# Two-layer hybrid mixer on one core: layer 1's input stage moved into the block of layer 0's output projection

## The chip, the cores and the metric

One core of a Trainium2 chip runs the whole program in one launch. The metric is the device time of one execution in microseconds (us), lower is better. TensorE is called PE here, its weight loads PEld, VectorE DVE, ScalarE ACT, GpSimd POOL, and SyncE, which only issues transfers, SP.

## What is computed

Two layers run over 1152 tokens of 1024 channels: 1024 latent tokens and 128 context tokens. Attention and delta rule couple the tokens inside a layer. Cut to what matters here, a layer is:

```python
mod = (jnp.dot(jax.nn.silu(cond), w_mod) + b_mod)[:, None, :]
shift, scale, gate = jnp.split(mod, 3, axis=-1)
h = rmsnorm(x, norm_pre) * (1 + scale) + shift
z = jnp.einsum('bld,de->ble', h, w_in)        # 2832 columns
... pooling, attention and delta branches of z ...
y = jnp.einsum('ble,ed->bld', gates * branches, w_out)
x = x + gate * rmsnorm(y, norm_post)
```

`cond` is `c` for latent tokens and `c_ctx` for context tokens. It is an input, so the modulation of layer 1 does not depend on layer 0. `h` of a token depends only on that token's `x`, so the input stage of layer 1 can work on a tile of 128 tokens as soon as layer 0 has finished that tile.

## The kernel before

The tokens are 9 tiles of 128, and three groups of 384 (`GRP`). Every matrix product in f32 accuracy is made of three passes over a high and a low part (`split3`, lines 88 to 96), so one output unit of 128 channels by 384 tokens takes 8 blocks of the contraction times 3, 24 matmuls. Order is written out by hand: each engine runs its instructions in the order of the code and waits on semaphores.

A loop on the chip (`Fori`) runs over the two layers. A layer consists of two blocks, with a barrier and a clearing of semaphores after each:

* `enter` (line 114), the input stage. SP loads the x tiles (`load_x`: from the inputs for layer 0, from `out_y` in DRAM for layer 1, chosen by a branch) and four 2 MB blocks of `w_mod`, in the order of `LOADS`. For each tile, ACT squares and sums it (L683), POOL makes the reciprocal root (L283 to L285), DVE scales it (L446), PE turns it by 8 transposes (L562) and ACT copies it to `h_f32` (L691). In between PE multiplies the blocks of `w_mod` (`mod_product`, L547; each row is copied by DVE at L450 and turned by PE at L553). Only when shift and scale are there, DVE modulates (L458), ACT rounds the high part (L696) and DVE subtracts the low part (L465); PE starts the products of `w_in` behind the first low part. Those go through 11 chunks of columns (`CHUNKS`). The first four chunks have 6 units each, numbered n = 0 to 23; the token-major chunks follow with 9 units each, and then 24 gate units. ACT empties each unit from PSUM (L719 and others) out of a ring of six banks. The last two blocks of `w_mod` (the gate vector) are products 4 and 5: PE does them behind units 3 and 8, and their turns behind unit 13 (`extra`). They share one buffer `wg`. DVE splits each weight chunk (L361, L363) and does the six convolutions (L370, L373).
* `mix_and_project` (line 775): delta rule, scan, attention, and `project_out` (line 1819). There PE runs 48 matmuls of 512 columns for each token tile (L2015). ACT squares and sums the result (L1942), POOL makes the root (L1962, L1964), DVE scales by root and gate (L1983), POOL adds x (L1968), and SP stores the tile to `out_y`. The last tile is done in two halves (L1937, L1939, L1978, L1981).

`io["y"]` has a place for each layer, so layer 1 loads in `enter` what layer 0 stored, and loads it once more in `project_out` for the addition.

## Time and profile before

| what | us |
|---|---|
| median of 3 runs | 1774.92 |
| lowest and highest of them | 1767.24, 1775.39 |
| the profiled execution's own time | 1763.57 |
| its span, first to last instruction | 1761.9 |
| PE busy | 1640.4 (93% of the span) |
| DVE, POOL, ACT busy | 1000.7, 923.4, 622.0 |
| PE's last product of layer 0 ends | about 872.5 from the start |
| PE's first `w_in` product of layer 1 starts | 935.19 from the start |

The span is read in order: layer 0's input stage from 5 to 348, its delta rule, scan and attention to about 770, its output projection to 877, and then layer 1 with the same stages. Only one core runs. The profiled execution was 11 us shorter than the median of the runs, so a sum made against the trace has to be moved before it is compared with a median.

### The profile page before, as it was taken

The page shows a single profiled execution, that of the slowest core. Times are in us where ns is not written, and L with a number is a line of the kernel's source. Part 1 is how long each engine was busy: PE and PEld are TensorE (multiplying, and loading weights), DVE is VectorE, ACT ScalarE, POOL GpSimd, SP SyncE. Part 2 cuts the span into 40 slices and gives each one's busy share as a digit, 9 for nine tenths or more (in the row PEclk, how much of TensorE's full clock was granted, in tenths as well). Part 3 has the DMA queues.
Part 4 walks back from the last instruction along what each step waited for, and adds up shares of the span by engine and source line. Part 5 has one row for each costly group of instructions (what it writes and reads, how often), then busy time and mean ns, then how long its engine had stood idle before and what let it go on. Part 6 is the DMA issues. An engine that isn't in the chain of part 4 may idle for free. (4 is left out here: it accounts for less than half of the span.)

```text
span 1761.9 us, 40485 instructions
## 1 busy us (share of the span) xinstructions
PE 1640.4 (93%) x17250; PEld 1342.9 (76%) x17250; DVE 1000.7 (57%) x1472; ACT 622.0 (35%) x1260; POOL 923.4 (52%) x856
## 2 busy tenths in 40 slices
PE   4999999989989999999849999999999899999998
PEld 2899999979976555558628999999799765555586
DVE  2672246377746767791126722463777477677911
ACT  4412321144444444561143123211444444445611
POOL 1003594089944878852210035940899448788522
PEclk8999999999999999999969999999999999999999
DMA  9312013110000001032292220131100000010322
GB/s 335 112 68 77 25 62 102 54 41 22 4 12 14 7 26 33 26 138 100 80 321 102 74 77 25 61 102 55 42 22 4 12 14 7 26 33 26 138 99 81
DMA packets 71246, 117.22 MB, mean 67 GB/s; under 512 B 10128, under 2 KB 42128, under 8 KB 71056
## 3 DMA queue, kind: packets, MB, share of 16 engines
q1 hardware_dynamic: 70128, 114.18, 19.1%
q8 instruction: 140, 2.29, 0.5%
q10 hardware_dynamic: 928, 0.34, 0.1%
q14 instruction: 50, 0.41, 0.1%
HBM read 95.03 MB, written 19.47 MB: 65 GB/s over the span
## 5 line engine op out<-in xcount | busy, mean ns | idle before, releaser
L1439 POOL TENSOR_TENSOR attn_accp<-attn_accp,attn_pr 128x1024 f32<-128x1024 f32 x110 | 269.4, 2449 | 42.3 <-ACT attn_pr L1505 36.6
L93 PE MATMUL ps<-h_hi,in_w_hi 128*128 128x384 f32 x768 | 261.0, 340 | 5.0 <-DVE h_lo L465 4.9
L94 PE MATMUL ps<-h_lo,in_w_hi 128*128 128x384 f32 x768 | 259.3, 338 | 0.0
L95 PE MATMUL ps<-h_hi,in_w_lo 128*128 128x384 f32 x768 | 259.1, 337 | 0.0
L1709 DVE TENSOR_REDUCE attn_ql<-ps 128x1 f32<-128x1152 f32 x128 | 172.6, 1355 | 102.3 <-PE ps L1627 102.0
L1505 ACT ACTIVATE attn_pr<-ps 128x512 f32<-128x512 f32 x292 | 158.7, 595 | 170.7 <-PE ps L1671 162.0
L93 PEld LDWEIGHTS ps<-h_hi,in_w_hi 128*128 128x128 f32 x768 | 145.0, 189 | 10.1 <-issue 6.7
L1670 PEld LDWEIGHTS ps<-attn_QH,attn_KH 128*128 128x128 f32 x292 | 55.5, 190 | 122.1 <-ACT attn_pr L1505 55.2
L94 PEld LDWEIGHTS ps<-h_lo,in_w_hi 128*128 128x128 f32 x768 | 145.2, 189 | 0.0
L95 PEld LDWEIGHTS ps<-h_hi,in_w_lo 128*128 128x128 f32 x768 | 145.1, 189 | 0.0
L1680 PE MATMUL ps<-attn_pr,z 128*64 128x512 f32 x520 | 139.5, 615 | 0.0
L919 POOL TENSOR_TENSOR delta_ML<-delta_EK,local 128x256 f32<-128x256 f32 x180 | 130.6, 746 | 14.2 <-PE ps L957 13.5
L1670 PE MATMUL ps<-attn_QH,attn_KH 128*128 128x512 f32 x292 | 131.5, 450 | 0.0
L93 PE MATMUL ps<-in_w_hi,h_hi 128*128 128x256 f32 (+1 forms) x432 | 124.1, 287 | 0.0
L95 PE MATMUL ps<-in_w_hi,h_lo 128*128 128x256 f32 (+1 forms) x432 | 122.7, 284 | 0.0
L94 PE MATMUL ps<-in_w_lo,h_hi 128*128 128x256 f32 (+1 forms) x432 | 122.5, 283 | 0.0
L957 PE MATMUL ps<-delta_TR,delta_ML 64*64 64x64 f32 x2880 | 111.0, 221 | 11.0 <-POOL delta_ML L919 5.0
L1671 PE MATMUL ps<-attn_QL,attn_KO 65*128 65x512 f32 x292 | 116.2, 398 | 0.0
L297 POOL TENSOR_TENSOR in_scratch<-zz 128x1175 f32<-128x1175 f32 x4 | 8.6, 2144 | 201.2 <-ACT zz L721 201.2
L957 PEld LDWEIGHTS ps<-delta_TR,delta_ML 64*64 64x64 f32 x2880 | 97.3, 135 | 18.7 <-DVE delta_TR L1199 11.8
L1199 DVE TENSOR_TENSOR delta_TR<-delta_TR,ps 128x256 f32<-128x256 f32 x180 | 72.7, 404 | 52.2 <-PE ps L957 50.3
L1627 PE MATMUL ps<-attn_KH,attn_QH 128*128 128x384 f32 x384 | 89.6, 341 | 1.9 <-DVE attn_ql L1709 1.9
(251 smaller groups left out, 3581.3 us busy)
## 6 DMA issues: line engine op xcount, KB each, us to landing
in_w<-in_w_in SPq DMA_DIRECT2D x22, 1024.0 KB, 5.4
zz<-in_w_mod SPq DMA_DIRECT2D x8, 2048.0 KB, 12.9
gates<-in_gate SPq DMA_DIRECT2D x48, 192.0 KB, 1.9
z<-out_y SPq DMA_DIRECT2D x18, 512.0 KB, 5.2
attn_gt<-gates SPq DMA_DIRECT2D x34, 256.0 KB, 2.7
z<-in_x_sample SPq DMA_DIRECT2D x16, 512.0 KB, 5.2
z<-in_w_mod SPq DMA_DIRECT2D x4, 2048.0 KB, 10.1
out_w<-in_w_out SPq DMA_DIRECT2D x16, 512.0 KB, 6.0
```

The source lines that it names most:

```text
L93: nc.tensor.matmul(out, a_hi(i), b_hi(i), start=(i == 0), stop=False)
L94: nc.tensor.matmul(out, a_hi(i), b_lo(i), start=False, stop=False)
L95: last = nc.tensor.matmul(out, a_lo(i), b_hi(i), start=False, stop=(i == n - 1))
L919: nc.gpsimd.tensor_tensor(pairs(ML[d][:, i % 2]), EA[d][:, j % 3, :, 0], level_mask(i, d), ALU.mult).then_inc(ml_done, 1)
L957: last = nc.tensor.matmul(heads(bank, off)[rows(c), h, :], lhs(rows(c), h), rhs(rows(c), h), start=True, stop=True)
L1439: nc.gpsimd.tensor_tensor(acc, a, pr[:, n % 4], ALU.add).then_inc(pool_added, 1)
L1505: nc.scalar.activation(pr[:, n % 4, e], ps[:, e, :], ACT.Exp, scale=HD ** -0.5).then_inc(p_done, 1)
L1627: last = nc.tensor.matmul(ps[:, bank + c, 0:GRP], QH[:, p % 3, blk // 2, col:col + P], KH[:, g, GRP * c:GRP * c + GRP], start=True, stop=True)
L1670: nc.tensor.matmul(ps[:, e, :], KH[:, g, ks], QH[:, p % 3, e, :], start=True, stop=False)
L1671: nc.tensor.matmul(ps[:, e, :], KO[0:HD + 1, g, ks], QL[0:HD + 1, p % 2, e, :], start=False, stop=True).then_inc(st_done, 1)
L1680: nc.tensor.matmul(ps[HD * e:HD * e + HD, 2 + p % 2, :], values(p, kt, e), pr[:, n % 4, e], start=(kt == 0), stop=(kt == STEPS_OF[p] - 1)) ...
L1709: nc.vector.tensor_reduce(ql[:, a % 4, blk, HD:HD + 1], ps[:, bank:bank + 3, 0:GRP], AX_XY, ALU.max).then_inc(mx_read, 1)
```

## The change

The loop over the layers is written out in Python. Layer 0 still has an input block of its own (`enter`, l = 0). Layer 1's input stage becomes a set of functions which run in the block of layer 0's `project_out`, as `nxt`:

* While PE multiplies tile t of layer 0's output projection, tile t - 2 is turned. ACT squares the finished y tile where it lies in SBUF, POOL makes the root, DVE scales it into one buffer `xn`, PE does its 8 transposes inside product t (behind block k = 1; in the last product behind block k = 3 of the first half), and ACT copies it to the h buffers. DVE modulates group 0 behind tile 3 and group 1 behind tile 6. The first weight chunk of layer 1 is loaded at tile 3 and split behind tile 4.
* Shift, scale and gate of layer 1 are made in layer 0's input stage: products 6 to 11 of 2 MB blocks of `w_mod`, one behind each of the units 10, 13, 16, 19, 21 and 23, through the one buffer `wg`. The turns go behind units 9, 15, 20 and 25. Product 5 moves from unit 8 to unit 7.
* Layer 1's first chunk is done as `side_by_side`: for each block k, both channel blocks of a token group. The high and low parts are made only after the last output product, since they lie where its operands lay. The last two tiles are turned inside groups 0 and 1, and the two halves of the last y tile are scaled and added between low parts. ACT instead of DVE rounds the high part of chunk 1.
* Layer 1 no longer loads y in its input stage, nor `w_mod`.

```diff
-    names = " ".join(f"x{i}" for i in range(1, len(ap.shape)))
-    return ap[bass.ds(l, 1)].rearrange(f"a {names} -> (a x1) {names[3:]}" if len(ap.shape) > 2 else "a x1 -> (a x1)")
+    return ap[l]
...
+GATE_PRODUCTS = {3: 4, 7: 5}
+NEXT_PRODUCTS = {10: 6, 13: 7, 16: 8, 19: 9, 21: 10, 23: 11}
+COLUMN_TURNS = {9: 4, 15: 6, 20: 8, 25: 10}
...
+    def x_square(act, t):
+        if l == 0:
+            act.wait_ge(x_in[t % X_RING], 16 * (t // X_RING + 1))
+            act.drain()
+            src, junk = x[:, t % X_RING, :], sq
+        else:
+            before["tile_added"](act, t)
+            if t >= 1:
+                act.wait_ge(x_turned, t)
+            src, junk = before["y"][t % 2], xn[:]
+        nc.scalar.activation(junk, src, ACT.Square, accum_out=ss[:, t:t + 1]).then_inc(summed, 1)
+    def x_root(pool, t):
+        pool.wait_ge(summed, t + 1)
+        nc.gpsimd.tensor_scalar(rsq[:, t:t + 1], ss[:, t:t + 1], 1.0 / D, EPS, ALU.mult, ALU.add)
+        pool.drain()
+        nc.gpsimd.tensor_tensor(rsq[:, t:t + 1], rsq[:, t:t + 1], m["mhalf"][:, 0:1], ALU.pow).then_inc(root, 1)
+    def x_scale(dve, t):
+        dve.wait_ge(root, t + 1)
+        if l == 0 and t >= 2:
+            dve.wait_ge(x_turned, t - 1)
+        src = x[:, t % X_RING, :] if l == 0 else before["y"][t % 2]
+        nc.vector.tensor_scalar(xn_tile(t), src, rsq[:, t:t + 1], None, ALU.mult).then_inc(scaled, 1)
+    def x_scaled(eng, t):
+        eng.wait_ge(scaled, t + 1)
+    def x_turn(pe, t):
+        pe.wait_ge(scaled, t + 1)
+        if t >= 2:
+            pe.wait_ge(x_copied, t - 1)
+        for k in range(KD):
+            last = nc.tensor.transpose(x_banks(t)[:, k, :], xn_tile(t)[:, P * k:P * k + P], m["ident"])
+        last.then_inc(x_turned, 1)
+    def x_copy(act, t):
+        act.wait_ge(x_turned, t + 1)
+        tk = slice(P * t, P * t + P)
+        nc.scalar.activation(h_raw(slice(0, KD), tk), x_banks(t), ACT.Copy).then_inc(x_copied, 1)
+    def modulate(dve, g, k):
+        if l:
+            dve.wait_ge(x_copied, 3 * g + 3)
+        for tk, c in h_parts(g):
+            last = nc.vector.tensor_scalar(h_raw(k, tk), h_raw(k, tk), m["scale"][:, l, k, c:c + 1],
+                                           m["shift"][:, l, k, c:c + 1], ALU.mult, ALU.add)
+        last.then_inc(modulated, 1)
...
+        def gate_weights(n):
+            part, half = divmod(n % 6, 2) if n >= 6 else (2, n - 4)
+            if n >= 5:
+                sp.wait_ge(mod_mm, n)
+            c0 = D * part + 512 * half
+            sp.dma_start(wg, w_mod[n // 6][:, :, c0:c0 + 512]).then_inc(wg_in, 16)
...
+            sp.wait_ge(scaled, NT)
+            gate_weights(4)
+            gate_weights(5)
+            weights(2)
+            gate_weights(6)
+            gate_weights(7)
+            weights(3)
+            gate_weights(8)
+            gate_weights(9)
+            weights(4)
+            gate_weights(10)
+            gate_weights(11)
+        else:
+            weights(1)
+            before["last_stores"](sp)
+            weights(2)
+            weights(3)
+            weights(4)
...
+        else:
+            for k in range(KD):
+                low_part(0, k)
+                if k in (2, 3):
+                    last_half(k - 2)
+            x_scale(dve, NT - 1)
+            for k in range(KD):
+                low_part(1, k)
+            groups = (2,)
+        for g in groups:
...
+        def beside(*rows):
+            for n, columns in rows if l == 0 else ():
+                next_columns(n) if columns else mod_row(n)
+        split(1)
+        beside((4, False))
+        dve.wait_ge(padded, 1)
+        split(2)
+        beside((5, False))
+        convolve(0)
+        convolve(1)
+        beside((4, True), (6, False))
+        convolve(2)
+        split(3)
+        beside((7, False))
+        convolve(3)
+        beside((6, True))
+        convolve(4)
+        beside((8, False))
+        convolve(5)
+        beside((9, False))
+        split(4)
+        beside((8, True), (10, False), (11, False), (10, True))
+        split(5)
+        for t in range(NT):
...
+        def extra(n):
+            if l == 0 and n in GATE_PRODUCTS:
+                mod_product(GATE_PRODUCTS[n])
+            if l == 0 and n in COLUMN_TURNS:
+                first = COLUMN_TURNS[n]
+                pe.wait_ge(mod_copied, first + 2)
+                mod_turn(first, 7)
+                mod_turn(first + 1, 7)
+            if l == 0 and n in NEXT_PRODUCTS:
+                mod_product(NEXT_PRODUCTS[n])
...
+        def side_by_side(g):
+            _, hi, lo = w_parts(0)
+            tk = slice(GRP * g, GRP * g + GRP)
+            if g == 0:
+                before["last_but_one_scaled"](pe)
+            elif g == 1:
+                before["all_added"](pe)
+            else:
+                pe.wait_ge(x_copied, NT - 1)
+            for k in range(KD):
+                pe.wait_ge(h_done, KD * g + k + 1)
+                for a in range(2):
+                    out, ch = ps[:, ring(2 * g + a), 0:GRP], slice(P * a, P * a + P)
+                    nc.tensor.matmul(out, hi[:, k, ch], h_hi[:, k, tk], start=(k == 0), stop=False)
+                    nc.tensor.matmul(out, hi[:, k, ch], h_low(k, tk), start=False, stop=False)
+                    last = nc.tensor.matmul(out, lo[:, k, ch], h_hi[:, k, tk], start=False, stop=(k == KD - 1))
+                    if k == KD - 1:
+                        last.then_inc(product, 1)
+                if g < 2 and k == 1:
+                    x_turn(pe, NT - 2 + g)
+        n = 0
+        for i, (c0, cols, kind) in enumerate(CHUNKS):
...
+        else:
+            before["all_multiplied"](act)
+            for k in range(5):
+                high_part(0, k)
+            x_square(act, NT - 1)
+            for k in range(5, KD):
+                high_part(0, k)
+            x_copy(act, NT - 2)
+            for k in range(6):
+                high_part(1, k)
+            x_copy(act, NT - 1)
+            for k in range(6, KD):
+                high_part(1, k)
+            raw, hi, _ = w_parts(1)
+            act.wait_ge(w_in[1], landed(1))
+            nc.scalar.activation(hi[:, :, 0:WC], raw[:, :, 0:WC], ACT.Copy).then_inc(w1_high, 1)
+            for k in range(KD):
+                high_part(2, k)
...
                 act.wait_ge(y_out[t % 2], 16 * (t // 2))
+                if nxt:
+                    nxt["x_scaled"](act, t - 2)
...
+        if nxt:
+            nxt["x_square"](act, 0)
         for t in range(1, NT):
             squares(t)
+            if nxt and t < NT - 1:
+                nxt["x_copy"](act, t - 1)
+                nxt["x_square"](act, t)
...
+            if nxt and t == 2:
+                nxt["vector_loads"](sp)
+            if nxt and t == 3:
+                nxt["first_load"](sp)
+        if nxt is None:
+            last_stores(sp)
+            stored(sp)
...
+        if nxt:
+            nxt["x_scale"](dve, 0)
+        for t in range(1, NT - 1):
             scale(t)
+            if nxt:
+                nxt["x_scale"](dve, t)
+            if nxt and t in (3, 6):
+                for k in range(KD):
+                    nxt["modulate"](dve, t // 3 - 1, k)
+            if nxt and t == 4:
+                nxt["first_split"](dve)
+        if nxt:
+            nxt["vector"](dve, last_half)
+        else:
+            last_half(0)
+            last_half(1)
...
+                        if nxt and i == 0 and k == 3:
+                            nxt["x_turn"](pe, t - 2)
...
+                if nxt and t >= 2 and k == 1:
+                    nxt["x_turn"](pe, t - 2)
...
-        with nc.Fori(0, DEPTH) as l:
+        for l in range(DEPTH):
+            more = enter_memory(nc, m, l + 1) if l + 1 < DEPTH else None
...
+                mix_and_project(nc, io, m, l, more)
```

On PE, in the product of the last token tile of layer 0 and what follows it. Before, the rows end with the last block's matmuls and the block's end (L856 is a branch to it); L2015 is the output product.

```order
L2015 MATMUL ps<-out_w_lo,out_b_late 128x512
L2015 MATMUL ps<-out_w_hi,pbr_lo 128x512
L856 UNCONDITIONAL_BRANCH
L2088 REGISTER_ALU
L2088 COMPARE_AND_BRANCH
```

Now the first product of layer 1 follows in the same block, with one tile's transposes (L321, `x_turn`) after two blocks k, that is, twelve matmuls (L802 to L804, `side_by_side`).

```order
L2295 MATMUL ps<-out_w_lo,out_b_late 128x512
L2295 MATMUL ps<-out_w_hi,pbr_lo 128x512
L802 MATMUL ps<-in_h_hi,first_hi 128x384
L803 MATMUL ps<-in_h_early_lo,first_hi 128x384
L804 MATMUL ps<-in_h_hi,in_first_w_lo 128x384
```

Behind twelve of these, PE has the rows

```order
L804 MATMUL ps<-in_h_hi,in_first_w_lo 128x384
L321 MATMUL ps<-masks,out_xn 128x128 x8
L802 MATMUL ps<-in_h_hi,first_hi 128x384
L803 MATMUL ps<-in_h_early_lo,first_hi 128x384
L804 MATMUL ps<-in_h_hi,in_first_w_lo 128x384
```

The block's end went from behind the last output product to behind the whole input stage of layer 1.

On DVE, at the end of layer 0's output projection. Before (L1983 scales a tile, L1978 and L1981 scale and add a half of the last):

```order
L1983 SCALAR_TENSOR_TENSOR z<-ps,out_rs,zz 128x1024 x7
L1978 SCALAR_TENSOR_TENSOR z<-ps,out_rs,zz 128x512
L1981 TENSOR_TENSOR z<-z 128x512
L1978 SCALAR_TENSOR_TENSOR z<-ps,out_rs,zz 128x512
L1981 TENSOR_TENSOR z<-z 128x512
```

Now (L2239, L2247 and L2250 are these three; L311 scales a y tile for layer 1, L333 modulates, L615 makes a low part):

```order
L2239 SCALAR_TENSOR_TENSOR z<-ps,out_rs,zz 128x1024
L311 TENSOR_SCALAR out_xn<-z,out_rsq_next 128x1024
L333 TENSOR_SCALAR in_h_late<-in_h_late,scale,shift 128x384 x8
L2239 SCALAR_TENSOR_TENSOR z<-ps,out_rs,zz 128x1024
L311 TENSOR_SCALAR out_xn<-z,out_rsq_next 128x1024
L615 TENSOR_TENSOR in_h_early_lo<-in_h_early,in_h_hi 128x384 x3
L2247 SCALAR_TENSOR_TENSOR z<-ps,out_rs,zz 128x512
L2250 TENSOR_TENSOR z<-z 128x512
L615 TENSOR_TENSOR in_h_early_lo<-in_h_early,in_h_hi 128x384
L2247 SCALAR_TENSOR_TENSOR z<-ps,out_rs,zz 128x512
L2250 TENSOR_TENSOR z<-z 128x512
L615 TENSOR_TENSOR in_h_early_lo<-in_h_early,in_h_hi 128x384 x4
```

The scaling and modulating of layer 1 moved between the tiles of layer 0, and the last tile's halves now stand between low parts that PE waits for.

## Rows read from the trace of the kernel before

**Rows 1.** Busy times by stretch: stretch, length, PE, PEld, DVE, ACT, POOL, PEclk, DMA share, GB/s.

```profile
872.50:884.40 11.90, 0.00 (x1) 0.00 (x0) 2.80 (x4) 0.69 (x2) 0.93 (x3) 0.69 0.13 49
884.40:893.20 8.80, 0.00 (x0) 0.00 (x0) 0.00 (x0) 2.65 (x4) 1.31 (x4) 0.50 0.73 190
893.20:935.19 41.99, 26.46 (x169) 17.03 (x169) 14.71 (x22) 18.67 (x27) 6.38 (x22) 0.78 1.03 379
935.19:938.21 3.02, 3.02 (x10) 3.02 (x11) 3.02 (x8) 1.74 (x4) 0.00 (x0) 0.50 0.01 5
938.21:964.70 26.49, 26.42 (x154) 24.05 (x154) 22.19 (x49) 11.77 (x25) 0.00 (x0) 1.00 0.01 2
```

**Rows 2.** ACT in order of time: start, length, instruction, [idle before it <- releaser].

```profile
872.54 0.60 ACT L1939 ACTIVATE z<-ps 128x512 f32<-128x512 f32 x1 [4.85 <-PE ps L2015]
...
964.70 0.38 ACT L719 ACTIVATE zz<-ps 128x256 f32<-128x256 f32 x1 [3.62 <-PE ps L95]
...
973.05 0.49 ACT L719 ACTIVATE zz<-ps 128x384 f32<-128x384 f32 x1 [3.68 <-PE ps L95]
977.22 0.38 ACT L719 ACTIVATE zz<-ps 128x256 f32<-128x256 f32 x1 [3.68 <-PE ps L95]
...
983.48 0.49 ACT L719 ACTIVATE zz<-ps 128x384 f32<-128x384 f32 x1 [3.38 <-PE ps L95]
...
1000.18 0.49 ACT L719 ACTIVATE zz<-ps 128x384 f32<-128x384 f32 x1 [3.68 <-PE ps L95]
1006.17 0.38 ACT L719 ACTIVATE zz<-ps 128x256 f32<-128x256 f32 x1 [5.50 <-PE ps L95]
```

**Rows 3.** PE in order of time: transposes, and the first products of layer 1.

```profile
916.50 1.94 PE L562 MATMUL ps<-masks,z 128*128 128x128 f32 x16
...
935.65 0.52 PE L94 MATMUL ps<-h_lo,in_w_hi 128*128 128x384 f32 x1
935.97 0.52 PE L95 MATMUL ps<-h_hi,in_w_lo 128*128 128x384 f32 x1
```

**Rows 4.** One y tile of layer 0: squared by ACT, added by POOL; the next.

```profile
816.88 1.03 ACT L1942 ACTIVATE z<-ps 128x1024 f32<-128x1024 f32 x1 [10.03 <-PE ps L2015]
...
820.37 2.41 POOL L1968 TENSOR_TENSOR z<-z 128x1024 f32<-128x1024 f32 x1 [1.40 <-DVE z L1983]
...
828.02 1.03 ACT L1942 ACTIVATE z<-ps 128x1024 f32<-128x1024 f32 x1 [10.03 <-PE ps L2015]
```

**Rows 5.** One x tile of layer 1: squared by ACT, scaled by DVE.

```profile
891.03 1.06 ACT L683 ACTIVATE in_scratch<-z 128x1024 f32<-128x1024 f32 x1 [0.98 <-DMA z<-out_y]
...
893.20 0.75 DVE L446 TENSOR_SCALAR z<-z,in_rsq 128x1024 f32<-128x1024 f32 x1 [15.68 <-POOL in_rsq L285]
```

**Rows 6.** DVE at the last y tile's halves.

```profile
874.58 0.75 DVE L1978 SCALAR_TENSOR_TENSOR z<-ps,out_rs,zz 128x512 f32<-128x512 f32 x1 [9.72 <-POOL out_rs L1964]
875.40 0.69 DVE L1981 TENSOR_TENSOR z<-z 128x512 f32<-128x512 f32 x1
```

**Rows 7.** Low part, high part and a weight split in layer 1.

```profile
935.35 0.55 DVE L465 TENSOR_TENSOR h_lo<-h_f,h_hi 128x384 fp32r<-128x384 f32 x1
935.47 0.53 ACT L696 ACTIVATE h_hi<-h_f 128x384 fp32r<-128x384 f32 x1 [0.60 <-DVE h_f L458]
...
958.17 2.29 DVE L363 TENSOR_TENSOR in_w_lo<-in_w,in_w_hi 128x2048 fp32r<-128x2048 f32 x1
```

**Rows 8.** Transfers issued between 884 and 1000: size, median us from issue to landing.

```profile
zz<-in_w_mod SPq DMA_DIRECT2D x4, 2048.0 KB, 14.1
...
z<-in_w_mod SPq DMA_DIRECT2D x2, 2048.0 KB, 10.0
```

**Rows 9.** PE around a short pause in attention.

```profile
552.32 0.68 PE L1609 MATMUL ps<-masks,attn_ql 128*65 128x128 f32 x4 [1.54 <-DVE attn_ql L1709]
...
553.66 0.63 PE L1670 MATMUL ps<-attn_QH,attn_KH 128*128 128x512 f32 x1
...
556.44 0.39 PE L1671 MATMUL ps<-attn_QL,attn_KO 65*128 65x512 f32 x1
```

More of the change, by code:

```diff
@@ new lines, in enter @@
+    cleared, csil_done, mod_mm, mod_copied, mod_turned = (
+        sem(n) for n in ("cleared", "csil_done", "mod_mm", "mod_copied", "mod_turned"))
+    summed, root, scaled, x_turned, x_copied = (sem(n) for n in ("summed", "root", "scaled", "x_turned", "x_copied"))
+    modulated, h_high, h_done, columns_read = (sem(n) for n in ("modulated", "h_high", "h_done", "columns_read"))
+    w_in = [sem(f"w_in{i}") for i in range(2)]
+    w1_high = sem("w1_high")
+    g_out = [sem(f"g_out{i}") for i in range(3)]
@@ new lines, in enter, with in_h @@
+    inv_in, inv_used, rope_in = sem("inv_in"), sem("inv_used"), sem("rope_in")
+    ps, h_hi, z, zc, zu = m["ps"], v["h_hi"], m["z"], m["zc"], m["zu"]
+    w_dram = layer(io["w_in"], l).rearrange("(k p) n -> p k n", p=P)
+    w_mod = [layer(io["w_mod"], i).rearrange("(k p) n -> p k n", p=P) for i in range(DEPTH)]
+    NB = 6
+    convw = m["convw"][l]
+    def in_h(whole, k, tk):
+        if l == 0:
+            return v[whole][:, k, tk]
+        if tk.stop <= GRP:
+            return v[whole.replace("h", "h_early", 1)][:, k, tk]
+        return v[whole.replace("h", "h_late", 1)][:, k, tk.start - GRP:tk.stop - GRP]
@@ new lines, in xn_tile, with units, products_before @@
+    def xn_tile(t):
+        return xn[:, t % 2, :] if l == 0 else xn[:]
+    def units(kind, cols, first=False):
+        if kind == "tokens":
+            return [(t, None) for t in range(NT)]
+        if kind == "delta" and first:
+            return [(b, g) for g in range(T // GRP) for b in range(2)]
+        return [(b, g) for b in range((cols + P - 1) // P) for g in range(T // GRP)]
+    def products_before(i):
+        return sum(len(units(kind, cols)) for _, cols, kind in CHUNKS[:i])
+    first_of = {kind: products_before([k for _, _, k in CHUNKS].index(kind)) for kind in ("pool", "tokens")}
@@ L1566, in scalar @@
                 out["weights_high"](act, 0)
[L1567 removed]
+        out["scalar"](act, lambda: evict(("sum", len(PAIRS) - 1)), nxt)
     def turn_start(pe, item):
```

1288 lines of the change are left out of this document (670 added, 618 removed).

## The prediction

> **What bounds the kernel now.** I read the busy times of the page first: PE is busy 93% of the span, so a change pays only where PE idles, or runs at its lower clock, or is given other work. The busy times by stretch then show the one long hole that this change touches [rows 1]. From 872.50, where layer 0's last output product ends, PE does nothing for 20.7 us: 11.90 of these are the tail of the last tile, the barrier and the clearing, 8.80 the first loads of layer 1. From 893.20 to 935.19 it has 26.46 us of work in 41.99, with the DMA engines full (share 1.03, 379 GB/s): the stretch waits for y tiles and for 2 MB blocks of `w_mod`. Even then it starts the products of `w_in` at 1.2 GHz (granted clock 0.50 for 3.02 us) before it is back at 2.4 GHz.
>
> ACT's order of time gives two marks that do not move with the code [rows 2]: the square of the last half tile starts at 872.54, as the last output product ends, and unit 5 of layer 1 is emptied at 964.70. So 92.2 us pass for work that is 6 units of PE. A unit takes 4.17 us at full clock, the distance between 973.05 and 977.22 [rows 2]; six are 25.0 us. Behind the first four chunks PE stays the bound, until the input stage ends.
>
> **What goes: layer 1's way from one mark to the other.** I rebuild it from rows, with E the end of the last output product.
>
> *To the first matmul.* ACT squares the half (0.60, and about 0.2 to read the sum), rounds the first high part (0.53) and DVE subtracts the low part (0.55) [rows 2, 7]. With the semaphores between them PE starts at E + 2.1. Nothing can hide this: the h buffers lie where the product's operands were.
>
> *Group 0.* PE needs 6 matmuls per block k, 1.04 us at 0.174 each (4.17/24). DVE is in code order: low parts 0 to 2 are done at E + 3.1; then the first half tile, whose root is there at 874.58, E + 2.1, takes 1.43 us with its addition, from 874.58 to the next at 876.01 (0.75, 0.69 and a drain) [rows 6]; then low part 3, the second half until about E + 6.6, and low part 4. ACT stands behind that half too: it squares the tile (1.06 plus 0.2) [rows 5] from E + 6.7 to E + 7.9 and only then rounds high parts 5 to 7. Low part 5 is ready at about E + 9.1, when PE would want it at E + 8.3, because one tile's transposes (0.97 us: 16 in 1.94) [rows 3] stand behind block 1. Group 0 ends at E + 12.2.
>
> *Groups 1 and 2.* Group 1 costs 8 x 1.04 + 0.97 = 9.3 us: its high and low parts are made ahead of PE, and what ACT does between fits (two tile copies and a weight cast of 2048 columns, an estimated 4 us from the 1.06 for 1024 columns of a square [rows 5]). In group 2 DVE has to modulate and subtract by turns; before this ran at 1.05 us per block, PE's own pace. It ends at E + 29.9. I add 1.0 us for a drop of the clock (below), and 0.3 because DVE's subtraction of chunk 1 (2.29) [rows 7] comes after its last low part. So about 31.2 us stand where 92.2 stood: **61.0 us gained**. The bounds are 25.0 + 2.1 + 1.9 = 29.0, with no wait but the first, and the case of the clock priced as a rival.
>
> *Behind it.* Product 5 of layer 1 shows as 983.48 - 977.22 - 4.17 = 2.09 us on PE, its two turns as 1006.17 - 1000.18 - 4.17 = 1.82 [rows 2]. Both vanish from layer 1: **3.9 us gained**.
>
> **What comes: modulation in layer 0.** Six products and three pairs of turns are put between units in which PE is the bound: 6 x 2.09 + 3 x 1.82 = **18.0 us lost**, with nothing that covers them. In the hole they stood beside loads. Moving product 5 from unit 8 to 7 costs nothing in the sum, nor do the row copies on DVE: by my count convolution 5 ends some 10 us before the first tile's turn asks for it.
>
> Do the loads keep up? `wg` is a single buffer, so load n is issued when product n - 1 is over. From there to product n, PE has 3 units (12.5 us) before products 7 and 9, 3 units and turns (14.3) before 6 and 8, 2 units and turns (10.2) before 10, and 2 units (8.3) before 11. A block lands after 10.0 us in this kind of stretch and after 14.1 in the crowded one [rows 8]. At 10.0 only product 11 waits, 1.7 us: **1.7 us lost**. Bounds: 0, if a load that runs alone lands sooner, and 1.6 + 1.6 + 3.9 + 5.8 = 12.9 at 14.1. I take 10.0, since layer 0 has the same neighbours (one 1 MB weight chunk). SP is held behind these waits: the table of window counts and chunk 5 are issued some 25 us later. POOL's windows need the table, but its next work waits for turned tiles, which PE now delivers about 18 us later, and it had 10 us to spare.
>
> **What comes: turning inside the output product.** Seven tiles (0 to 6) are turned there: 7 x 0.97 = **6.8 us lost** on a PE that is full. The chain before a turn is hidden. A tile takes 11.14 us on PE (816.88 to 828.02), and is added at 822.78, 5.9 behind its product [rows 4]; the square, root and scaling take 893.20 + 0.75 - 891.03 = 2.9 us [rows 5], 8.8 in all, some 9.2 with ACT's order. The turn is asked for in the product after next, behind block 1: 11.14 + 0.97 + 2.8 = 14.9. Spare 5.7 us per tile. The 16 modulations (each a little less than a low part's 0.55 [rows 7]) and the first split end before DVE's next tile, within a us of it at tiles 3 and 6. A late one would delay the bank, which PE wants only a tile later. In the rest of the program instructions and sizes are the same.
>
> **The clock.** A pause of 1.54 us in attention is followed by matmuls of 512 columns at 0.63 us for some 3.5 us before they are at 0.39 [rows 9]. So my pause of 2.1 us may bring 1.2 GHz for 3 us. In those, PE does half as much, but group 0 contains 0.8 us of waits anyway, hence the 1.0 us above. The Trainium skill ("TensorE: Matmul & The Clock Gate", "A second HAM failure mode: psum-queue depth-cycling") speaks against the change: a PE that micro-idles between groups of matmuls falls back to half rate and warms up again, over and over. By that rule group 0 and what follows would run slow throughout, not 3 us.
>
> **The sum.** 61.0 + 3.9 - 18.0 - 1.7 - 6.8 = 38.4 us gained against the trace, 1763.57 - 38.4 = 1725.2. The four executions of before (three runs and the profiled one) average 1770.3, the median given is 1774.92, the profiled one lowest. A new median of three may fall anywhere in that spread, so I count from the average: 1770.3 - 38.4 = **1732 us**.
>
> **The rivals.**
>
> *Loads of `w_mod` lag* (0.12). If they land after 14.1 us as in the crowded stretch [rows 8], 12.9 us go instead of 1.7: gain 27.2, 1743. For it: SP holds them in one order with weight chunks. Against: in that stretch the engines were full for 42 us [rows 1], in layer 0 behind unit 7 they carry 3 MB per 25 us.
>
> *The clock stays low through units 0 to 5* (0.08). A matmul of 384 columns then starts every 0.32 us (935.65 to 935.97) [rows 3], 144 of them take 46.1 us, with two slow turns (3.9) and the 2.1 us: 52.1 instead of 30.9, gain 17.2, 1753. For it: PE waits for a low part at most blocks of group 0. Against: from 938.21 on PE ran the same pieces at clock 1.00 with short waits [rows 1]. This is the time that the skill's rule would give.
>
> *The y chain becomes the bound, and it is slower* (0.04). Place: the seven turns that stand in PE's order inside the product. ACT copies tile t - 1 before it squares tile t, so a late turn delays the next square and the lateness is handed on. Each us by which the chain is longer than 14.9 costs 7. From 20.4 us per tile on (5.5 x 7 = 38.4) all is lost, from 21.7 it is slower by over 0.5%, and at 23 us it stands at 1732 + 57 = 1789. Against it: 9.2 us from rows, and the engines on it are idle two thirds of each tile. DVE's new work could stretch POOL's addition, but not by 11 us.
>
> *The gain is lost later* (0.04). If something other than PE set layer 1's input stage behind unit 5, an early start would only wait: within 9 us of before, say 1768. Against: PE is full there, and the convolutions start 5 us earlier against PE than before.
>
> **How the numbers follow.** The forecast has 0.72. Its own range is 1722 (1763.57 less 41.1, with no wait for loads and no drop of the clock, is 1722.5) to 1742 (the median 1774.92 less 38.4, and 5 us of error in waits that I placed by hand). For 8 in 10 I go on to the lagging loads counted from the average and some way towards the median, 1749, and down to 1720. A measurement of this kernel can tell about 0.5%, 9 us, from no change. Faster by more: forecast, loads and clock, 0.92; within: 0.04; slower: 0.04.
>
> **What would show it.** In the changed profile: the square of the last half tile, then PE's first `w_in` product 2 us later, and the emptying of unit 5 some 31 us behind the square, or a little more since ACT has high parts before it. PE's mean at 0.97 us per turned tile and a tile period of 12.1 us in layer 0's output product against 11.1 in layer 1's. Six intervals longer by 2.1 us among units 10 to 23 of layer 0, the last by 3.8. Granted clock 1.00 from E + 5 on. I would be wrong if PE waits for scaled tiles inside the output product, if product 10 waits for its load, if DVE is more than 1 us behind PE in group 2, or if layer 1's later stages begin less than 60 us earlier behind E.

## The result, and the profile after

| | before | changed |
|---|---|---|
| median of 4 runs, us | 1771.54 | 1729.47 |
| lowest and highest | 1767.24, 1775.39 | 1724.64, 1731.94 |
| profiled execution: own time, span | 1763.57, 1761.9 | 1731.49, 1729.7 |
| PE busy | 1640.4 (93%) | 1637.1 (95%) |

The changed kernel takes 0.9756 of the time before (95% interval 0.9729 to 0.9782), 42 us less. The forecast was 1732.

The two profiled executions differ by 32 us only; where the other 10 are is told under "Profile against profile" and in "Why the prediction was right". First the stretch that the change is about. ACT in order of time, the marks of [rows 2] in the changed kernel (start, length, instruction, idle before it and releaser):

```profile
903.53 0.60 ACT L2197 ACTIVATE z<-ps 128x512 f32<-128x512 f32 x1 [4.36 <-PE ps L2295]
904.12 2.16 ACT L878 ACTIVATE in_h_hi<-in_h_early 128x384 fp32r<-128x384 f32 x5
909.54 1.06 ACT L298 ACTIVATE out_xn<-z 128x1024 f32<-128x1024 f32 x1 [3.26 <-DVE z L2250]
...
910.60 1.34 ACT L878 ACTIVATE in_h_hi<-in_h_early 128x384 fp32r<-128x384 f32 x3
...
932.97 0.38 ACT L938 ACTIVATE zz<-ps 128x256 f32<-128x256 f32 x1
```

The last half tile is squared at 903.53, unit 5 is emptied at 932.97: 29.4 us where 92.2 were. PE in the same stretch:

```profile
905.39 0.42 PE L802 MATMUL ps<-in_h_hi,first_hi 128*128 128x384 f32 x1 [1.89 <-DVE in_h_early_lo L615]
905.64 0.34 PE L803 MATMUL ps<-in_h_early_lo,first_hi 128*128 128x384 f32 x1
...
907.58 1.03 PE L321 MATMUL ps<-masks,out_xn 128*128 128x128 f32 x8
...
911.43 0.33 PE L804 MATMUL ps<-in_h_hi,in_first_w_lo 128*128 128x384 f32 x1
911.77 0.45 PE L802 MATMUL ps<-in_h_hi,first_hi 128*128 128x384 f32 x1
```

One pause of 1.89 us, one tile's turns in 0.8 us of PE's order (907.40 + 0.17 to 908.37), and one hitch: 911.77 comes 0.34 behind 911.43 where 0.17 is the pace, because low part 5 is late. The busy times by stretch answer to [rows 1]:

```profile
903.50:905.60 2.10, 0.21 (x1) 0.24 (x2) 0.94 (x2) 2.07 (x6) 1.00 (x3) 1.00 0.41 117
905.60:915.00 9.40, 9.39 (x56) 9.04 (x56) 8.09 (x16) 6.14 (x14) 1.07 (x9) 1.00 0.79 252
915.00:925.00 10.00, 10.00 (x62) 9.96 (x61) 6.07 (x17) 5.79 (x9) 0.00 (x0) 1.00 0.01 4
925.00:933.00 8.00, 8.00 (x48) 8.00 (x47) 7.88 (x15) 4.25 (x12) 0.00 (x0) 1.00 0.01 3
```

PE (second number) is full from 905.6 on and the granted clock stays 1.00. What comes in exchange stands in layer 0. ACT's emptying of units 7, 8 and 9, and of 22 to 25 (L938 a block of channels, L924 a token tile):

```profile
93.54 0.49 ACT L938 ACTIVATE zz<-ps 128x384 f32<-128x384 f32 x1 [3.68 <-PE ps L96]
99.80 0.38 ACT L938 ACTIVATE zz<-ps 128x256 f32<-128x256 f32 x1 [5.77 <-PE ps L96]
103.98 0.49 ACT L938 ACTIVATE zz<-ps 128x384 f32<-128x384 f32 x1 [1.42 <-PE ps L96]
...
174.12 0.49 ACT L938 ACTIVATE zz<-ps 128x384 f32<-128x384 f32 x1 [5.77 <-PE ps L96]
...
178.30 0.39 ACT L938 ACTIVATE zz<-ps 128x256 f32<-128x256 f32 x1 [2.63 <-PE ps L96]
...
183.37 0.38 ACT L924 ACTIVATE z<-ps 128x256 f32<-128x256 f32 x1 [4.52 <-PE ps L96]
...
186.40 0.38 ACT L924 ACTIVATE z<-ps 128x256 f32<-128x256 f32 x1 [2.57 <-PE ps L96]
```

A plain unit takes 4.17 to 4.18; 99.80 - 93.54 = 6.26 holds a product, 2.09 us. So does 174.12 behind unit 21 (167.86), which is product 10, and 183.37 - 178.30 = 5.07 against 3.03 for a plain token unit is product 11: neither waits for its load. The profile's page has the reason (transfer, count, KB each, median us to landing), 8.0 us where I had taken 10.0:

```profile
z<-in_w_mod SPq DMA_DIRECT2D x8, 2048.0 KB, 8.0
```

In layer 0's output projection a tile now takes 12.01 us, against 11.14 [rows 4]. The squares of three tiles:

```profile
867.50 1.03 ACT L2200 ACTIVATE z<-ps 128x1024 f32<-128x1024 f32 x1 [4.94 <-PE ps L2295]
...
879.52 1.03 ACT L2200 ACTIVATE z<-ps 128x1024 f32<-128x1024 f32 x1 [4.94 <-PE ps L2295]
...
891.53 1.03 ACT L2200 ACTIVATE z<-ps 128x1024 f32<-128x1024 f32 x1 [4.94 <-PE ps L2295]
```

**Profile against profile.** Marks from the two traces, in us, changed minus before: PE's first `w_in` product +2.2 (55.64 against 53.43); the end of layer 0's input stage +20.1; the first chained product of the delta rule +20.7 (381.52 against 360.85); its scan's end +24.7, so the delta stage itself is 4.0 longer (181.1 against 177.1); the last output product +31.0; the first chained product of layer 1 -35.1 (1207.58 against 1242.72); its scan's end -32.0 (3.1 longer again); the end -32.2. The change touches neither delta stage. In layer 0's the granted clock differs; here the end of layer 0's scan, in a window of the changed kernel and the same work in the kernel before:

```profile
520.00:545.00 25.00, 20.54 (x528) 18.13 (x524) 8.44 (x23) 8.59 (x21) 4.92 (x8) 0.86 0.07 18
```

```profile
497.00:521.00 24.00, 19.34 (x592) 17.25 (x584) 9.45 (x28) 9.50 (x23) 6.30 (x10) 1.00 0.05 13
```

The first has a granted clock of 0.86 and 528 matmuls in 25 us, the second 1.00 and 592 in 24. The first experiment asks whether the change brings that.

### The profile page after: what moved, and what is told of

Same layout as the page of the kernel before. It is cut to its first block and busy times, and to the rows that moved or that the text cites. A ratio compares the mean times of both kernels' runs of the same rounds, so it can differ in the third digit from the quotient of the medians.

```text
span 1729.7 us, 40122 instructions
## 1 busy us (share of the span) xinstructions
PE 1637.1 (95%) x17250; PEld 1343.1 (78%) x17250; DVE 1001.0 (58%) x1471; ACT 621.3 (36%) x1260; POOL 924.0 (53%) x854
## 5 line engine op out<-in xcount | busy, mean ns | idle before, releaser
L94 PE MATMUL ps<-in_h_hi,in_w_hi 128*128 128x384 f32 x720 | 244.1, 339 | 2.5 <-DVE in_h_lo L615 2.5
L96 PE MATMUL ps<-in_h_hi,in_w_lo 128*128 128x384 f32 x720 | 242.4, 337 | 0.0
L94 PEld LDWEIGHTS ps<-in_h_hi,in_w_hi 128*128 128x128 f32 x720 | 135.7, 188 | 9.3 <-issue 7.5
L96 PEld LDWEIGHTS ps<-in_h_hi,in_w_lo 128*128 128x128 f32 x720 | 135.5, 188 | 0.0
L95 PE MATMUL ps<-in_h_lo,in_w_hi 128*128 128x384 f32 x384 | 129.6, 338 | 0.0
L94 PE MATMUL ps<-in_w_hi,in_h_hi 128*128 128x256 f32 (+1 forms) x432 | 124.2, 288 | 0.0
L95 PE MATMUL ps<-in_w_lo,in_h_hi 128*128 128x256 f32 (+1 forms) x432 | 122.4, 283 | 0.0
L1354 ACT ACTIVATE delta_X<-ps 128x256 f32<-128x256 f32 x180 | 68.8, 382 | 64.4 <-PE ps L1184 60.4
L1184 PE MATMUL ps<-delta_X,delta_TR 64*64 64x64 f32 x2304 | 86.4, 222 | 1.4 <-issue 0.7
L931 ACT ACTIVATE in_gate<-ps 128x384 f32<-128x384 f32 x48 | 23.4, 492 | 174.6 <-PE ps L96 93.7
```

Source lines behind the costliest of these rows:

```text
L94: nc.tensor.matmul(out, a_hi(i), b_hi(i), start=(i == 0), stop=False)
L95: nc.tensor.matmul(out, a_hi(i), b_lo(i), start=False, stop=False)
L96: last = nc.tensor.matmul(out, a_lo(i), b_hi(i), start=False, stop=(i == n - 1))
L1184: last = nc.tensor.matmul(heads(bank, off)[rows(c), h, :], lhs(rows(c), h), rhs(rows(c), h), start=True, stop=True)
```

## The experiments

**The changed kernel again.** No edit.

> The changed kernel once more, unaltered. The forecast's account: the way from the last output product of layer 0 to the emptying of unit 5 of layer 1 stays 29.4 us within 0.5, the output product's tile period 12.0 us, the six products of layer 1's modulation 2.1 us each; the time 1724 to 1733 us. In the first profile of it the two delta stages together were about 6 us longer than in the profile of before, beside stretches with granted clock 0.50. If these come by chance, they lie elsewhere in this profile and the stages' lengths change by some us; if the change causes them, they come back at the same place and size (both last scans 2.3 to 2.6 us longer than before).

Measured: 1727.63 (1725.6 to 1731.51), ratio 0.9765 (0.9746 to 0.9784). E to unit 5 is 29.44 us again (900.39 to 929.83), the output tile 12.01, the six intervals in layer 0 longer by the same 2.1. The delta stages take 178.6 and 177.4 us, against 181.1 and 180.7 in the first profile, and the end of the scan in layer 0 runs at 1.00:

```profile
519.00:544.00 25.00, 20.34 (x618) 18.12 (x613) 10.28 (x29) 9.92 (x24) 6.89 (x11) 1.00 0.06 14
```

618 matmuls in 25 us where the first profile had 528 in the same length. The kernel that only writes out the loop (next) shows the same lower clock there (0.80 in a window of 25 us, and 181.3 us), so the 7 us of the delta stages are not the change's: they come in some executions and not in others. What decides it I did not test.

**The loop alone.** The kernel before, with

```diff
-        with nc.Fori(0, DEPTH) as l:
+        for l in range(DEPTH):
...
-    with eng.If(l):
-        eng.dma_start(dst, layer(io["y"], (l + (DEPTH - 1)) % DEPTH)[t * P:t * P + P, :]).then_inc(done, 16)
-    with eng.Else():
-        eng.dma_start(dst, src).then_inc(done, 16)
+    if l:
+        src = layer(io["y"], l - 1)[t * P:t * P + P, :]
+    eng.dma_start(dst, src).then_inc(done, 16)
```

> The kernel before, with its loop over the two layers written out, so that layers have addresses fixed at build, no branch in the loads and no jump back; nothing else of the change. My account: the gain comes from what is joined at the boundary, and the loop costs next to nothing: within 0.3% of before, the hole behind the last output product of layer 0 still over 90 us up to unit 5. Rival: loop and addresses cost a good part of the 20.7 us in which PE does nothing there, and of every stage's start: then 8 to 15 us faster than before.

Measured: 1764.85, ratio 0.9964 (0.9947 to 0.9980). Between my account (within 0.3%) and the rival (8 to 15 us): 5 to 6 us. The hole up to unit 5, which I had put over 90 us, is 86.4 (877.40 to 963.84). PE's first `w_in` product comes 56.8 us behind the start of the last output product, against 63.1 before. The rows around the boundary, first of the kernel before, then of this one:

```profile
876.83 0.69 DVE L1981 TENSOR_TENSOR z<-z 128x512 f32<-128x512 f32 x1
884.41 0.32 POOL L279 MEMSET z<- 128x256 f32 x1 [9.87 <-issue]
...
885.08 1.41 SPq L234 DMA_DIRECT2D cols<-in_cols  x1
```

```profile
881.70 0.69 DVE L1980 TENSOR_TENSOR z<-z 128x512 f32<-128x512 f32 x1
885.28 0.32 POOL L278 MEMSET z<- 128x256 f32 x1 [5.88 <-POOLq L77]
...
885.68 0.43 SPq L233 DMA_DIRECT2D cols<-in_cols  x1
```

From the last addition's start to the next layer's first instruction pass 7.6 us with the loop and 3.6 without; the 4.0 us between them are the jump back and what follows it, and the issue of a transfer at an address from a register takes 1.41 instead of 0.43. The Trainium skill ("Runtime: NRT & Kernel Launch", "Instruction fetch mechanics") says that a taken branch out of the prefetched pages has to fetch its target first; a gap of 9.87 us on POOL that ends by nothing but "issue", where the other kernel has one of 5.88, agrees with it, but no run here separates the fetch from the rest.

**Modulation alone.** The loop written out and layer 1's modulation in layer 0, but layer 1's input stage in its own block, loading y from memory. From the changed kernel:

```diff
-            more = enter_memory(nc, m, l + 1) if l + 1 < DEPTH else None
...
-                mix_and_project(nc, io, m, l, more)
+                first = enter(nc, io, m, l, part, enter_memory(nc, m, l))
...
+                mix_and_project(nc, io, m, l, None)
...
-        src = x[:, t % X_RING, :] if l == 0 else before["y"][t % 2]
+        src = x[:, t % X_RING, :]
```

> One half of the change alone: the loop is written out and layer 1's modulation is worked out in layer 0 as in the changed kernel, but layer 1's input stage stands in a block of its own and loads its y tiles from memory, as before. In the kernel with the loop written out PE's first w_in product of layer 1 comes 56.8 us behind the mark E. My account: 12 MB of w_mod are gone from the hole; left are 8 us to the first instruction, 5 to the first loaded tile, nine tiles at ACT's pace (a square of 1.25 and a copy of 1.0, 20 us) and the modulation of a group: E + 38, that is 19 us less, and 3.9 behind it, against 18.0 more in layer 0: 5 us below the written out kernel, 1760. So the modulation's move pays next to nothing by itself, and the tiles kept on the chip bring the other 30 us or more. Rival: the loads of w_mod were what the hole waited for, so the first product comes at E + 28 or sooner and half of the change brings half of the gain (1750 or less).

Measured: 1759.95, ratio 0.9938 (0.9921 to 0.9956), the time that my account had. The first `w_in` product comes 41.0 us behind the start of the last output product, 3 us later than I had it, and far from the rival's 28. The stretches behind E:

```profile
897.50:905.50 8.00, 0.00 (x1) 0.00 (x0) 2.80 (x4) 0.69 (x2) 0.93 (x3) 0.77 0.17 66
905.50:911.00 5.50, 0.00 (x0) 0.00 (x0) 0.00 (x0) 0.00 (x0) 0.00 (x0) 0.50 0.67 187
911.00:938.10 27.10, 14.69 (x72) 12.96 (x73) 11.80 (x15) 19.81 (x29) 9.28 (x24) 0.67 0.64 220
```

8 us of tail and barrier, 5.5 for the first tile to land, and then ACT is the busiest engine with 19.81 of 27.10, while the DMA share is down from 1.03 [rows 1] to 0.64; that ACT now sets the pace is my reading of these shares. So taking 12 MB out of layer 1's input stage (8 of them loaded ahead of its first product) buys 15.8 us up to the first product (56.8 to 41.0) and 22.3 by the end of layer 1's input stage, and pays 18 for them. On its own that half of the change is worth 5 us by the medians (1764.85 and 1759.95, with intervals that overlap a little). The other half needs it: with `w_mod` in the way there would be nothing to join.

**Two blocks.** The changed kernel, cut at E by a meeting of all engines:

```diff
                 attn["vector"](dve, out, nxt)
+        if nxt:
+            with nc.Block() as block:
+                @block.sync
+                def _(sp):
+                    nxt["sync"](sp)
...
+                @block.vector
+                def _(dve):
+                    nxt["vector"](dve, lambda i: out["last_half"][0](i, dve))
```

> The changed kernel, but its joined block is cut at the last output product: all engines meet there, and layer 1's part of the last tile, its high and low parts and its products stand in a block of their own. The turned and modulated tiles stay on the chip. My account: what counts is that tiles 0 to 6 are ready and that the first weights are split, and the meeting itself costs what stood between the last addition and the first instruction in the kernel with the loop written out, 2.9 us, on top of POOL's root, which ends 1.9 us after the mark E. PE's first product of w_in then stands at about E + 6 in place of E + 2.3, unit 5 is emptied at E + 33, and the time is 3 to 5 us above the changed kernel's. Rival: that no engine stops is what makes the gain, because ACT and DVE lose their lead: then group 0 and group 1 wait as well and unit 5 comes at E + 38 or later.

Measured: 1731.41, ratio 0.9786 (0.9757 to 0.9816). PE:

```profile
900.14 0.39 PE L2310 MATMUL ps<-out_w_hi,pbr_lo 128*128 128x512 f32 x1
904.22 0.41 PE L802 MATMUL ps<-in_h_hi,first_hi 128*128 128x384 f32 x1 [3.69 <-DVE in_h_early_lo L615]
```

The pause is 3.69 us instead of 1.89, and unit 5 is emptied 32.5 us behind E (900.56 to 933.09) instead of 29.4; here 1.3 of the 3.1 go with a drop of the clock (below), which the joined block has in some profiles too. Behind the meeting PE waits for nothing up to unit 5. My account stands, with a cheaper meeting: PE starts 4.1 us behind the start of the last output product, not 6. So the meeting itself costs 1.8 us in the trace, and 2 to 4 us by the medians (1731.41 against 1729.47 and 1727.63), which the runs hardly resolve, since the intervals overlap. That the tiles are on the chip, turned and modulated, when E comes, is worth what lies between the last two kernels, 1760 against 1731. The two differ also in the side-by-side order of the first chunk and in ACT's rounding of chunk 1, and no run separates these.

**A longer pause.** One wait more on PE:

```diff
             if g == 0:
                 before["last_but_one_scaled"](pe)
+                pe.wait_ge(h_done, 5)
```

> The changed kernel with one wait more: PE begins layer 1's first product only when five low parts of group 0 are there, not one. Its pause at the mark E grows from 2.3 to about 6.6 us, and the short wait for low part 5 (0.34) goes. My account: PE falls behind by 4.4 us and by what a clock of 0.50 for some 3.4 us costs (0.95 where it fell in other profiles), so unit 5 is emptied at E + 33.8 to 34.8. [...]

Measured: 1736.28, ratio 0.9821 (0.9792 to 0.9850); unit 5 at E + 36.2 (901.27 to 937.48). PE and the stretches:

```profile
908.00 0.66 PE L803 MATMUL ps<-in_h_hi,first_hi 128*128 128x384 f32 x1 [6.77 <-DVE in_h_early_lo L615]
908.46 0.52 PE L804 MATMUL ps<-in_h_early_lo,first_hi 128*128 128x384 f32 x1
```

```profile
908.00:915.00 7.00, 7.00 (x31) 6.91 (x32) 0.00 (x0) 1.53 (x4) 0.19 (x1) 0.66 0.62 190
915.00:930.00 15.00, 15.00 (x90) 14.97 (x89) 10.43 (x26) 9.80 (x18) 0.82 (x7) 1.00 0.00 0
```

The pause grew by 4.9 us, unit 5 comes 6.8 later; the rest, 1.9 us, is the clock: behind 6.77 us of idleness PE's matmuls take 0.52 (1.2 GHz), and from 915 on the clock is 1.00 again. My range ended 1.4 us too early, 0.5 in the pause and 0.9 in the clock. A PE that stays at 1.2 GHz through units 0 to 5, the prediction's rival on the clock, is refuted at this size of pause: PE was back at 2.4 GHz within 7 us of work. Behind the short pause of the changed kernel both were seen: in its two profiles the clock stayed 1.00 and unit 5 came at 29.4, while the five variants without modulation, with six and with eight products gathered, and with the longer y chains (both below) had one drop each and came at 30.7 or 30.8 (893.26 to 923.98 in the second), with the same instructions there. So behind a pause of 1.89 us 0 or 1.3 us went with the clock, and the drop was the commoner case: five profiles of seven.

**No modulation of layer 1.** Left out: products 6 to 11, their loads and turns; layer 1 takes layer 0's columns.

```diff
-NEXT_PRODUCTS = {10: 6, 13: 7, 16: 8, 19: 9, 21: 10, 23: 11}
-COLUMN_TURNS = {9: 4, 15: 6, 20: 8, 25: 10}
+NEXT_PRODUCTS = {}
+COLUMN_TURNS = {9: 4}
```

> Left out: the modulation of layer 1 (six products of w_mod, their loads, three pairs of turns); layer 1 takes layer 0's columns. My account: these stand between products of an engine that is full and nothing covers them, so 6 x 2.09 + 3 x 1.82 = 18.0 us go, all of it in layer 0's input stage; time 1711 to 1712. Rival: part of them filled waits of PE (for emptied banks or for weights), or the 12 MB of loads cost the weight chunks something: then the stage is shorter by clearly less or more than 18 us (12 or 24).

Measured: 1710.73, ratio 0.9668 (0.9649 to 0.9687), 17 us below the changed kernel again. In the trace layer 0's products of `w_in` span 293.9 us, against 311.8 and 312.2 with modulation: 18.1 on average. The rival falls: no part was covered, and the loads cost the weight chunks nothing.

**Products gathered.** If 18 us are pure PE work, less of it is the way on. Each product puts its two useful rows elsewhere, all in one bank, and one set of turns serves them all:

```diff
-COLUMN_TURNS = {9: 4, 15: 6, 20: 8, 25: 10}
+COLUMN_TURNS = {9: 4, 25: 6}
...
             w = wm[n % 2] if n < 4 else wg
+            bank, c0 = (6 + n % 2, 32) if n < 6 else (6, 32 - 2 * (n - 6))
             for k in range(KD):
                 q = 32 * (k % 4)
-                last = nc.tensor.matmul(ps[q:q + 32, 6 + n % 2, :], csil[:, k, :], w[:, k, :], start=(k < 4), stop=(k >= 4))
+                last = nc.tensor.matmul(ps[q:q + 32, bank, :], csil[:, k, c0:c0 + 32], w[:, k, :],
+                                        start=(n <= 6 and k < 4), stop=(k >= 4 and (n < 6 or n == 11)))
```

> The changed kernel with all six products of layer 1's modulation gathered in one bank, each in rows of its own (the stationary operand is a window over zeros that puts its two columns elsewhere), one copy to SBUF and one set of four turns in place of three pairs. The same sums come out. My account: two pairs of turns go, 2 x 1.82 = 3.6 us, and the set of four matmuls costs half of a pair, 0.9 us less: 4.5 us in all, 1725 against 1729.5, in the trace layer 0's input stage 4.5 us shorter. Rival: each product now waits for nothing, but sums into one bank cost PE more than 2.09 us each, or the copy behind product 11 makes the single set of turns wait on PE (over 1 us at unit 25): then no gain.

Measured: 1723.33 (1716.21 to 1725.14), ratio 0.9729 (0.9706 to 0.9752); on the same chip the changed kernel took 1727.63. The stage spans 308.4 us, 3.6 less than the mean of the two above, not 4.5: a product here waited 0.6 us for its load, which nothing else delays any more. With products 4 and 5 gathered too:

```diff
-COLUMN_TURNS = {9: 4, 25: 6}
+COLUMN_TURNS = {25: 4}
```

> The changed kernel with all eight side products of layer 0 (4 to 11) gathered in one bank, each in two rows of its own, one copy and one set of four turns behind the last. Three pairs of turns go against the changed kernel, 3 x 1.82 = 5.5 us, and the set costs 0.9 less than a pair: 6.4 us in all, against 3.4 to 4.3 measured where six were gathered. Time 1722 where the changed kernel stands at 1728. Rival: layer 0's gate columns come 16 units later and the turns of the first token tile wait for them: no gain over the kernel with six gathered.

Measured: 1723.86, ratio 0.9741 (0.9725 to 0.9756). The stage spans 306.0 us, 6.0 less than in the changed kernel (expected 6.4) and 2.4 less than with six gathered. The times of the two gathered kernels can't be told apart; the profile of this one has a delta stage of 180.8 us where the other has 177.9. Either lies some 4 us below the changed kernel on the same chip (1727.63).

**A longer y chain.** Additions of 512 columns on POOL ahead of the root of each turned tile, 4 or 8 of them:

```diff
     def x_root(pool, t):
         pool.wait_ge(summed, t + 1)
+        if l and t < NT - 2:
...
+            for _ in range(4):
+                nc.gpsimd.tensor_tensor(spare[:], spare[:], spare[:], ALU.add)
+                pool.drain()
```

> The changed kernel with four additions of 512 columns ahead of each root of the turned tiles on POOL, an estimated 1.2 us each (a 1024 column addition takes 2.40), 4.8 us in all per tile 0 to 6. The profile shows 5.77 us between the end of a tile's scaling and its turn. My account: 4.8 is below it, so PE doesn't wait and the tile period stays 12.0 us. Rival (the y chain is near the bound): POOL's 2.4 us addition and its roots for the next tile are pushed back too, and PE waits at turns or for banks by 1 us per tile or more.

> The same with eight additions, an estimated 9.6 us per tile. My account: 3.8 us more than the chain has to spare, and POOL with 3.9 us of its own work per tile is over the period of 12.0, so PE waits at the turns, at least 3 us per tile: 20 to 30 us in all for seven tiles, E later by that against the end of the attention stage. Rival (the turns have two tiles' time, not one): every second turn waits only, 10 to 15 us in all.

Measured, one execution each: 1747.26 and 1777.05. Layer 0's output projection is 13.9 and 43.7 us longer than in the changed kernel. With four additions my account fell: it had no wait, and the rival's kind of wait came. With eight the waits came at all seven tiles as I had them (4.4 us each on average, over the 3 I had asked for), but the total lies far above my 20 to 30 us. PE waits for scaled tiles 8.3 us with four additions (the view of waits: total, times, longest), 30.8 us with eight:

```profile
PE ps L329 <- DVE out_xn L319: 8.3, 3, 4.1
```

```profile
PE ps L329 <- DVE out_xn L319: 30.8, 7, 8.8
```

The rest (5.6 and 12.9 us) goes with the clock, which falls behind these waits (four additions):

```profile
822.00:832.00 10.00, 6.29 (x22) 5.35 (x23) 4.12 (x4) 2.18 (x3) 6.80 (x7) 0.66 0.10 41
...
890.00:900.00 10.00, 7.38 (x24) 6.20 (x25) 2.04 (x2) 2.18 (x3) 6.66 (x8) 0.66 0.21 64
```

And the spare time is not the same at each tile. In the changed kernel, first tile 6, as it is scaled on DVE and turned on PE, then tile 0:

```profile
887.59 0.75 DVE L311 TENSOR_SCALAR out_xn<-z,out_rsq_next 128x1024 f32<-128x1024 f32 x1 [4.67 <-POOL out_rsq_next L304]
...
894.11 1.04 PE L321 MATMUL ps<-masks,out_xn 128*128 128x128 f32 x8
```

```profile
820.30 0.95 DVE L2259 TENSOR_TENSOR b_lo<-zz,out_b_late 128x768 fp32r<-128x768 f32 x1
821.17 0.74 DVE L311 TENSOR_SCALAR out_xn<-z,out_rsq_next 128x1024 f32<-128x1024 f32 x1
...
821.99 1.07 PE L321 MATMUL ps<-masks,out_xn 128*128 128x128 f32 x8
```

Tile 6 is scaled at 888.34 and turned from 894.11: 5.8 us to spare. Tile 0 stands on DVE behind the low parts of the output projection's late columns, is scaled at 821.91 and turned from 821.99: nothing to spare. The changed kernel sits on that edge with a wait of 0.2 us, of the first weight load.

Tile 0 is only the first of the three waits with four additions (4.1 us). The others, 1.56 and 2.63 us, stand at the turns of tiles 4 and 5, because of work that the change gave to DVE behind tiles 3 and 4, the modulations and the first split. DVE and PE with four additions:

```profile
863.12 3.21 DVE L341 TENSOR_SCALAR in_h_early<-in_h_early,scale,shift 128x384 f32<-128x384 f32 x8
866.23 1.29 DVE L2247 SCALAR_TENSOR_TENSOR z<-ps,out_rs,zz 128x1024 f32<-128x1024 f32 x1
...
877.75 1.09 PE L329 MATMUL ps<-masks,out_xn 128*128 128x128 f32 x8 [1.56 <-DVE out_xn L319]
...
892.62 1.97 PE L329 MATMUL ps<-masks,out_xn 128*128 128x128 f32 x8 [2.63 <-DVE out_xn L319]
```

In the changed kernel DVE is idle for 2.19 us behind those modulations and 1.81 us behind the split before the root of the next y tile is there. A chain 4.6 us longer uses that up: the next y tile is scaled late, and so is its copy for layer 1.

## Why the prediction was right

The total was met. In the order of its steps, each against the changed kernel's trace:

- **To the first matmul, and groups 0 to 2** (61.0 us gained, 31.2 left): 62.7, with 29.4 left. The path was as told: pause, three low parts, half tile, high parts 5 to 7 behind the last square. Two terms were too large. The clock (1.0 us) stayed at 1.00 in this profile, and fell in others for 1.3. The waits of group 0 (0.8) are one of 0.17: low part 5 was in time to within that, since ACT's square followed at E + 6.0, not 6.7.
- **Product 5 and its turns leave layer 1** (3.9): 3.5, as what E to the last `w_in` product gained (66.3) less the 62.7.
- **Modulation in layer 0** (18.0 lost): 17.9 and 18.3 in two profiles, and 17 to 18 when left out.
- **The wait for loads** (1.7 lost, bounds 0 to 12.9): 0. The block landed after 8.0 us, not 10.0; the price from the nearest row was 2 us too high. That the row's stretch had other neighbours may be why; no run shows it.
- **Turns inside the output product** (6.8 lost): 6.2, 0.89 a tile. The 0.97 was a misreading of [rows 3]: the 16 transposes ran at a granted clock of 1.00 and started 0.11 us apart (916.5 to 918.2), and their 1.94 us hold the tail of the last, 0.27 long. Eight at that pace are 0.9.

Measured so, the terms give 62.7 + 3.5 - 17.9 - 6.2 = 42.1, the medians 42.1; 38.4 had been the sum. That the two agree to a tenth is luck, since the executions of one kernel lie 6 to 10 us apart. Between the two profiles 2.2 us go for the later start of layer 0's `w_in`, 7.1 for the delta stages and 0.6 elsewhere, which leaves the 32.2. The sum had no term for the later start. Ten profiles of kernels with the modulation's move or derived from such a kernel have that start at 53.5 to 57.0 us, the two without it at 53.3 and 53.4; its cause is open. Counting from the average 1770.3 and not from the profiled 1763.57 was right: that execution of before was a short one, and 15 later ones had a median of 1770.12.

What was right only in total: I had booked the whole boundary as one stretch between two marks, so the loop never had a price. It has one, 5 to 6 us of the 42, and my account of that experiment put it near zero. By the four experiments the 42 us divide into 5 to 6 for the loop, 5 for the modulation's move net of its cost, 28 for tiles kept on the chip (net of their turns), and 2 to 4 for the joined block.

The rivals: the lagging loads did not come. The low clock through units 0 to 5, which I had priced as the time by the Trainium skill's rule on PE pausing between groups ("TensorE: Matmul & The Clock Gate", "A second HAM failure mode: psum-queue depth-cycling"), did not come at pauses of 1.89 us, nor at 6.77. The page of the Trainium skill itself speaks of falling back and warming up in turns, not of a clock that stays low, so my price was above its rule; one fall and one rise, as five of seven profiles had it, agree with it. The chain of y as bound did not come either, but my case against it was weak: "Spare 5.7 us per tile" does not hold for the first. I had looked at DVE's load at tiles 3 and 6, where I put the margin at one us (it is 2.2 behind tile 3, 1.8 behind the split at tile 4), and not at tile 0, where it is nil. And its price was too low: from 9.2 us more per tile my rule gives (9.2 + 9.2 - 14.9) x 7 = 24.5. Measured were 30.8 of waits, and 43.7 in all, with a granted clock of 0.87 over those 128 us.

## What to carry to other kernels

Work that moves into a stage where PE is full costs its full length there (18.1 us measured, 18.0 counted, against 22.3 gained by the move), so count every us of it, and then ask for less work, not for a better place. What paid at this boundary is that the next stage's operands are made before the last product ends (28 us); the meeting of all engines was worth 2 to 4. And when a chain is hidden behind a product, read its spare time at each tile, above all the first one, where its engine is still busy with the stage's own preparation, and those behind which the same engine was given more work.

## What the runs showed of the hardware

DVE and POOL slow each other. A low part of 768 columns takes DVE 0.95 us with POOL nearly idle (820.30 above), and 1.79 while POOL adds:

```profile
822.30 1.79 DVE L2267 TENSOR_TENSOR b_lo<-zz,out_b_late 128x768 fp32r<-128x768 f32 x1
```

```profile
816.89 6.38 POOL L308 TENSOR_TENSOR out_gap<-out_gap 128x512 f32<-128x512 f32 x4 [0.43 <-issue]
```

POOL's four additions took 6.38 us there and 4.60 where DVE was idle. The Trainium skill ("GPSIMD Engine Reference", "1. Specifications") says that POOL shares its SBUF interface with VectorE and contends with instructions of two SBUF inputs, which agrees. It means that the four additions were more than 4.6 us of delay at tile 0: they took 6.38 themselves, and DVE's low parts ahead of the scaling were stretched too.

The delta stage, the same instructions in every kernel, took between 177.1 and 182.5 us in the 24 stages of the profiles, and its length goes with its mean granted clock: 177.1 to 178.7 us at 0.99 or 1.00, 178.9 to 180.3 at 0.98, 179.9 to 181.3 at 0.97 or 0.96, and 182.3 to 182.5 at 0.95. The two profiles of the changed kernel differ by 5.8 us for that alone, a seventh of what this change is worth.
